# A skip term D times x moved from GpSimd to ScalarE in the second mixer of a hybrid decoder trunk

## The reference

```python
z, xbc, dt = split(h @ w_in)                 # z 2048, x 2048, B 1024, C 1024, dt 32
xbc = silu(causal_conv4(xbc) + conv_b)       # then split into x, B, C
# 8 groups of 4 heads of 64 features, state of 128
y = y_diag + y_off + d_skip[head] * x        # the last product is the skip term
y = y * silu(z)
y = rmsnorm(y, per group of 256) * g_norm
return y @ w_out
```

## Time and the profile before

| | |
|---|---|
| median of 3 runs | 1087.08 us (1086.83 to 1087.44) |
| profiled execution | 1086.96 us |
| its span | 1085.2 us, so 1.8 us lie around the span |
| PE busy | 1075.1 us, 99% |
| DVE busy | 787.6 us, 73% |
| ACT busy | 652.8 us, 60% |
| POOL busy | 87.2 us, 8% |
| granted TensorE clock | 0.998 of full |

### The profile page before, as it was taken

One profiled execution on the slowest core, in us unless ns is written; L12 is line 12 of the kernel. 1 busy time (PEld: TensorE's weight loads), 2 busy tenths in 40 slices (PEclk: granted clock), 3 DMA queues, 4 the chain that ended last, 5 costly groups with the idle time before them and its releaser, 6 DMA issues.

```text
span 1085.2 us, 17549 instructions
## 1 busy us (share of the span) xinstructions
PE 1075.1 (99%) x6399; PEld 940.1 (87%) x6399; DVE 787.6 (73%) x1122; ACT 652.8 (60%) x1002; POOL 87.2 (8%) x138
## 2 busy tenths in 40 slices
PE   9999999999999999999999999999999999999997
PEld 7888888899888888888888888899999988888886
DVE  5867667785677666667766767889888888776664
ACT  7645446784676445458454447697777797454453
POOL 3000000011010000000000000153222211000000
PEclk9999999999999999999999999999999999999999
DMA  9864655375357555474655554595555536655531
GB/s 283 296 230 156 206 180 145 107 241 183 121 163 245 193 190 197 155 233 140 232 192 193 177 171 121 173 289 184 187 155 155 170 121 213 238 171 195 196 112 40
DMA packets 162881, 199.30 MB, mean 184 GB/s; under 512 B 6372, under 2 KB 145856, under 8 KB 162832
## 3 DMA queue, kind: packets, MB, share of 16 engines
q1 hardware_dynamic: 160288, 190.86, 53.9%
q0 software_dynamic: 2384, 7.72, 2.1%
q10 hardware_dynamic: 160, 0.08, 0.0%
HBM read 197.56 MB, written 1.08 MB: 183 GB/s over the span
## 4 chain that ended last, share of the span: by engine, by line
PE 92%; ACT 3%; DMA 2%; DVE 2%; issue 1%; SPq 0%; POOL 0%; DVEq 0%; ACTq 0%; POOLq 0%
PE ps L1772 27%; PE ps L1934 24%; PE ps L1948 13%; PE ps L1826 9%; PE ps L1835 6%; PE ps L1738 5%; PE ps L1859 4%; DMA raw<-in_ffn_w_up 1%; PE ps L1798 1%; PE ps L2294 1%; PE ps L2153 0%; ACT exps L882 0%; PE ps L2298 0%; DVE xres L1179 0%; PE ps L1757 0%
## 5 line engine op out<-in xcount | busy, mean ns | idle before, releaser
L1224 DVE TENSOR_TENSOR ws<-raw,ws 128x1024 fp32r<-128x1024 f32 x180 | 213.3, 1222 | 139.7 <-ACT ws L685 139.7
L1772 PE MATMUL ps<-ws,hT 128*128 128x512 f32 x1320 | 314.0, 392 | 0.0
L685 ACT ACTIVATE ws<-raw 128x1024 fp32r<-128x1024 f32 x183 | 184.7, 1053 | 173.2 <-PE ps L1948 160.3
L1772 PEld LDWEIGHTS ps<-ws,hT 128*128 128x128 f32 x1320 | 243.7, 188 | 49.5 <-issue 1.1
L1934 PE MATMUL ps<-xT,ws 128*128 128x512 f32 x1152 | 267.3, 389 | 0.2 <-ACT ws L685 0.2
L1934 PEld LDWEIGHTS ps<-xT,ws 128*128 128x128 f32 x1152 | 216.1, 188 | 45.5 <-ACT ws L685 0.6
L1146 DVE TENSOR_TENSOR ws<-raw,ws 128x2048 fp32r<-128x2048 f32 (+1 forms) x88 | 197.2, 2243 | 27.8 <-ACT ws L599 27.8
L599 ACT ACTIVATE ws<-raw 128x2048 fp32r<-128x2048 f32 x83 | 157.6, 1909 | 2.6 <-PE ps L1772 2.6
L1948 PEld LDWEIGHTS ps<-xT,ws 128*128 128x128 f32 x1152 | 142.6, 192 | 2.5
L1948 PE MATMUL ps<-xT,ws 128*128 128x256 f32 x1152 | 144.1, 283 | 0.0
L1826 PE MATMUL ps<-xT,ws 128*128 128x256 f32 x960 | 119.2, 284 | 0.0
(11 more groups left out here) (263 smaller groups left out, 864.3 us busy)
## 6 DMA issues: line engine op xcount, KB each, us to landing
raw<-in_ffn_w_down SPq DMA_DIRECT2D x88, 512.0 KB, 4.8
raw<-in_ffn_w_gate SPq DMA_DIRECT2D x86, 512.0 KB, 4.0
raw<-in_ffn_w_up SPq DMA_DIRECT2D x86, 512.0 KB, 5.0
raw<-in_ssd_w_in SPq DMA_DIRECT2D x48, 512.0 KB, 4.7
raw<-in_gla_w_in SPq DMA_DIRECT2D x24, 512.0 KB, 4.8
raw<-in_ssd_w_out SPq DMA_DIRECT2D x16, 512.0 KB, 4.3
raw<-in_gla_w_out SPq DMA_DIRECT2D x8, 512.0 KB, 5.5
exps<-cs_rows POOLq DMA_DIRECT2D x8, 512.0 KB, 5.1
```

What stands on the lines that cost most here:

```text
L685: act.activation(ws[:, 0:2, 0, c], raw[:, 0:2, c], ACT.Copy).then_inc(gu_hi, 1)
L1224: dve.tensor_tensor(ws[:, 0:2, 1, c], raw[:, 0:2, c], ws[:, 0:2, 0, c].bitcast(F32), ALU.subtract).then_inc(gu_lo, 1)
L1772: mm = pe.matmul(ps[:, 2 * t + n, :], hT[:, par, j, a, t * P:(t + 1) * P], ws[:, slot, b, off:off + 512], start=(first and j + a + b == 0) ...
```

## The change

The two products per group that made `dx` on POOL are gone. ACT makes `dx` in four copies, one for each head, each over both tiles, with the head's D as the scale (`skips`). They stand between the evictions of B and of C for the groups scanned in bodies 2 to 7; in body 1 they stand after the eviction to `bcb`, in front of `hi` and the silu; in body 8 after `transposed`, in front of `gate_silu`. DVE's sum waits for the new semaphore `skipped`; `tok_mul` counts two products a group in place of four.

```diff
-                if not (isinstance(g, int) and g == 1):
-                    pool.wait_ge(y_out, 2 * (g - 1 + G))
-                for t in range(NT):
-                    pool.tensor_tensor(out=by_head(dx)[:, t], in0=by_head(xtok)[:, t],
-                                       in1=hb[:, 1, hs].rearrange("p (h o) -> p h o", o=1).broadcast_to([P, HPG, HD]),
-                                       op=ALU.mult).then_inc(tok_mul, 1)
...
-            def tiles_out(slot, count, banks, outs, done, scales=(1.0, 1.0)):
+            def tiles_out(slot, count, banks, outs, done, scales=(1.0, 1.0), between=None):
                 for c in range(2):
+                    if c == 1 and between is not None:
+                        between()
                     act.wait_ge(tile_mm[slot], count * 2 + c + 1)
...
+                    def skips():
+
+                        if not first:
+                            act.wait_ge(y_out, 2 * (g - 1 + G))
+                        act.wait_ge(tok_out, g - 1 + G + 1)
+                        for h in range(HPG):
+                            c = slice(h * HD, (h + 1) * HD)
+                            ins = act.activation(dx[:, :, c], xtok[:, :, c], ACT.Copy,
+                                                 scale=hb[:, 1, bass.ds((g - 1) * HPG + h, 1)])
+                        ins.then_inc(skipped, 1)
...
-                                  (1.0, 1.0) if ssd else RPRE)
+                                  (1.0, 1.0) if ssd else RPRE, skips if ssd else None)
...
                     if first and ssd:
+                        skips()
                         hi(SLOT_P1, g + n0[SLOT_P1] + 1)
                         gate_silu()
...
                         transposed(C)
                         if ssd:
+                            skips()
                             gate_silu()
...
-                                act.wait_ge(tok_mul, 4 * (g - 1))
+                                act.wait_ge(tok_mul, 2 * (g - 1))
...
-                            dve.wait_ge(tok_mul, 4 * g)
+                            dve.wait_ge(skipped, g)
...
-                            pe.wait_ge(tok_mul, 4 * (g - 1) + 2)
+                            pe.wait_ge(tok_mul, 2 * g)
```

More of the change, by code:

```diff
@@ L286, in trunk @@
         root_y = sem("root_y")
+        skipped = sem("skipped")
         root_step, root_pool = sem("root_step"), sem("root_pool")
@@ L1080, in body @@
                         act.wait_ge(tok_T, g + G + 1)
-                        act.wait_ge(tok_mul, 4 * g)
+                        act.wait_ge(tok_mul, 2 * g)
                         act.activation(xtok[:, :, :].rearrange("p t n -> p (t n)"), ps[:, E, :], ACT.Copy).then_inc(tok_out, 1)
```

## The result

The changed kernel takes 1088.83 us (median of 22 runs, 1088.42 to 1090.05) against 1087.08 us: a ratio of 1.0017, 95% interval 1.0011 to 1.0023. It is 1.75 us slower, where 1.9 us were forecast. The profiled execution took 1089.24 us with a span of 1087.5 us.

What follows compares the result with a forecast made beforehand. PE, busy 99% of the span, was taken to bound the kernel. Stalls of 1.08 us in body 1 and 0.86 us in the tail sum to 1.94 us, taking 1087.08 to 1089.0 us; range 1087.6 to 1090.2 us.

Steps and rivals of the forecast that it cites:

- Nothing to gain in the loop, nothing lost: Bodies 3 to 7: copies need 1.18 us of ACT's 2.49 us idle before tile C's eviction; cost 0.
- S: Time by which a group's four copies push ACT's following work: 1.18 us, bounds 1.08 and 1.55.
- Body 1: Copies in front of `hi` delay the eviction of tile B, for which PE's next tile waits: cost 1.08 us.
- Body 2: `bcb` about 0.35 us later relative to PE, POOL's masking earlier: cost taken as 0, bound 0.3 us.
- Tail: Copies before the table load delay the second square, and with it root, norm and transposes: cost 0.86 us.
- a gain from DVE's copy of the state: Tail: a quieter POOL may remove PE's 0.3 us wait for it, but the second square hangs on ACT: gives nothing.
- The sum: Whole kernel: 1.08 + 0.86 = 1.94 us slower, median 1087.08 becoming 1089.0 us, 0.18% slower.
- the end of the mixer moves by the sum of PE's waits: End of the mixer: the prediction is wrong if it moves by other than that sum.
- Rival 2: Copies don't overlap, or body 2 joins: S of 1.55 us gives 1089.8, with body 2's 0.3 us 1090.1; chance 0.23.
- rival 3: Copies hidden in body 1 or the tail: one alone gives 1087.9 to 1088.2 us, neither 1087.1; chance 0.15.
- rival 4: Relief of DVE from POOL's blocking reaches PE, its tail waits gone and copies hidden: 1086.6 us; chance 0.05.

Runs made afterwards that it cites:

- both_pool: Changed kernel with the skip term of groups 1 and 8 back on POOL, groups 2 to 7 by copies on ACT: 1087.15 us, ratio 1.0000.
- loop_seven: Changed kernel with seven more copies of the same shape and scale in each of bodies 3 to 6, into unused columns: 1088.83 us.
- imm_scale: Changed kernel with a constant scale of 1 in all copies, D left out of the skip term: 1088.05 us, ratio 1.0009.
- b1_pool: Changed kernel with group 1's skip term back on POOL, the other seven groups by copies on ACT: 1087.83 us, ratio 1.0006.
- tail_pool: Changed kernel with group 8's skip term back on POOL, the other seven groups by copies on ACT: 1088.25 us, ratio 1.0012.
- b1_plus2: Changed kernel with two more copies in body 1, into unused columns: 1089.45 us, ratio 1.0022.
- zf_late: Changed kernel with body 1's copy of zn to zf moved from ahead of the exponentials to between the evictions of B and C: 1088.02 us, ratio 1.0009.

## Why the prediction was right

- *Nothing to gain in the loop, nothing lost.* PE has 123.00 of 123.00 us in both profiles, and both_pool and loop_seven show it by time. The 12.2 us taken from POOL and 3.1 us from DVE are worth nothing.
- *S.* 1.18 us, worked out from the exponentials' spacing; measured 1.18. imm_scale shows that a pointer as scale carries 0.38 us of it.
- *Body 1.* Forecast 1.18 - 0.13 + 0.03 = 1.08 us; measured (720.42 - 718.91) - 0.46 = 1.05 us from the matmul behind the 25th load of the earlier trace rows, of which 0.07 come back at the next transposes, where PE used to arrive just before the features. b1_pool takes 1.00 us off the time.
- *Body 2.* Forecast 0, with 0.3 us as bound and ACT 0.35 us late at `bcb`; measured 0.29, no stall. The weights came out 0.83 us shorter, for which the prediction had no size. That POOL's earlier masking caused this is argued from the timeline and was not tried by itself.
- *Tail.* Forecast 0.86 us, measured 0.83 in the trace. By medians the tail is worth 0.58 us (against tail_pool) to 0.68 (b1_pool against both_pool). The traces say more than that: from PE's loads for the transposes of group 7's y to those of group 8's, it takes 8.15 us before, 8.98 after and 8.22 in tail_pool, so tail_pool takes back 0.76 us, and the rest of the difference to its median is inside the spread. The prediction dismissed a gain from DVE's copy of the state, since a later wait swallows it. That held: between 877 and 882 us PE loses 0.21 us in place of 0.51, comes 0.30 us earlier to the transposes for it, and stands there for 1.01 us, more than the 0.8 that the prediction expected to see.
- *The sum.* 1.94 us forecast, 1.05 - 0.07 + 0.83 = 1.81 in the trace, 1.75 by medians. The prediction set as a test that the end of the mixer moves by the sum of PE's waits: it moved by 2.26 - 0.46 = 1.80 us, and the new waits less the 0.30 us lost between 877 and 882 are 0.91 + 1.01 - 0.30 = 1.62 us by PE's matmuls, whose ends are modelled, and 1.91 by its weight loads (1.08 in body 1, 1.16 at the transposes, less 0.33 between 877 and 882). That holds to 0.2 us. Rival 2 (copies that don't overlap) and rival 3 (hidden work) fall with S and with the two waits; rival 4's relief is real for DVE, reaches PE only as those 0.30 us in the tail, and is swallowed there.

What was missed: that a longer stand can cost more than it lasts. With three copies more in body 1 (2.06 us in front of `hi` in place of 1.18) the clock dropped behind it in four of six executions, with two more in none of eleven, and no case of the prediction had that. The prediction's own bound, S = 1.55 us, would not have reached it: an estimated stand of 0.91 + 0.37 = 1.28 us, less than the 1.49 of b1_plus2.

## What to carry to other kernels

When one engine is busy nearly without a gap, moving work between the others can give back only what that engine still loses to waits, here 0.66 us between 704 and 890 us. Ask at each body of a pipeline written out by hand how much of the moved work fits between what the receiving engine owes to the first one. The loop's body says little about the first and the last: here the same four copies cost 0 in six groups, 1.0 us in the first and 0.6 to 0.8 us in the last. And keep an instruction that only has to be done some time, as the copy of `zn`, behind the eviction that another engine waits for: in zf_late that alone took back 0.8 us of what the change had cost. It was not tried in the kernel before, where PE doesn't wait for this eviction.

## What was unexpected of the hardware

A single stand of TensorE of 1.80 us, in a stretch in which it otherwise hardly waits, was followed by some 3 us at 0.50 of the clock, while one of 1.49 us left it at 1.00. By the mean clocks this came in four of six executions of that kernel and in none of eleven of the other. Where it came, it raised the price of three more copies from some 1.0 to 1.3 us to 2.2 to 2.5 us. A constant scale in place of a column shortens each copy of 128 elements on ScalarE from 393 to 303 ns (medians of 32).
